# Mixer and stick-breaking in a two-block transformer kernel: exponentials, copies and row norms in other places, a third score buffer

## The reference, cut to what matters

```python
# NSA: compressed, selected and window attention, 6 heads (not touched)
# stick-breaking, 4 heads, causal with s < t
z = (q @ k.T) * scale
log_rest = where(mask, log_sigmoid(-z), 0)
between  = reverse cumulative sum of log_rest, shifted by one
a = where(mask, exp(log_sigmoid(z) + between), 0);  o = a @ v
# HGRN2, 6 heads, chunk by chunk
b = cumsum(log_f);  decay[t, s] = exp(b[t] - b[s]) for s <= t
att = sum_d q[t,d] * key[s,d] * decay[t,s,d]
o = att @ v + (q * exp(b)) @ state
state = exp(b_last) * state + (key * exp(b_last - b)).T @ v
# all mixers: o * silu(gate), then
y = o @ w_out;  x = layer_norm(alpha * x + y) * ln_g + ln_b
```

## Time and profile before

| | us |
|---|---|
| median of 3 runs | 1365.36 |
| lowest, highest | 1359.78, 1369.44 |
| the profiled execution: time | 1365.65 |
| its span, first to last instruction | 1363.9 |
| TensorE busy (share of the span) | 1218.7 (89%) |
| TensorE weight loads | 677.9 (50%) |
| VectorE busy | 538.3 (39%) |
| ScalarE busy | 445.1 (33%) |
| POOL busy | 105.5 (8%) |

### The profile page before, as it was taken

How to read it: one execution, slowest core, us unless ns; L and a number is a source line. 1 busy time by engine, 2 the same in 40 slices (tenths; PEclk the granted TensorE clock), 3 DMA queues, 4 the chain that set the end, 5 groups by cost and what they waited for, 6 DMA issues and landing times.

```text
span 1363.9 us, 16366 instructions
## 1 busy us (share of the span) xinstructions
PE 1218.7 (89%) x5840; PEld 677.9 (50%) x5840; DVE 538.3 (39%) x1412; ACT 445.1 (33%) x1140; POOL 105.5 (8%) x138
## 2 busy tenths in 40 slices
PE   4899989999879898889999989989999899897865
PEld 1565634555554443344555555655454556544542
DVE  3335323334553211235543431112236632665555
ACT  0122324444441012232243312114243544563143
POOL 0000000000020000000000000000000000556342
PEclk8899999999889999989999989989998899888877
DMA  9311444580005302631001005241101111000001
GB/s 349 136 66 31 154 170 140 170 231 1 1 1 123 62 1 62 152 84 69 28 37 62 1 12 134 62 170 47 47 7 41 46 62 62 0 1 32 3 11 53
DMA packets 60406, 99.65 MB, mean 73 GB/s; under 512 B 12084, under 2 KB 22145, under 8 KB 60328
## 3 DMA queue, kind: packets, MB, share of 16 engines
q1 hardware_dynamic: 54514, 93.58, 22.2%
q10 hardware_dynamic: 5814, 5.04, 1.2%
HBM read 96.47 MB, written 4.08 MB: 74 GB/s over the span
## 4 chain that ended last, share of the span: by engine, by line
PE 77%; DVE 11%; ACT 5%; issue 2%; DMA 2%; ACTq 1%; POOL 1%; DVEq 0%; SPq 0%; POOLq 0%
PE PR L911 33%; PE OB L941 6%; PE SC L963 6%; PE PT L804 5%; PE PR L804 5%; PE OB L804 5%; PE SC L804 4%; PE PT L978 3%; PE PR L866 3%; DMA ring<-in_w_ada 2%; PE PR L1002 1%; DVE tok L1800 1%; DVE stage L1800 1%; POOL arena L1710 1%; DVE arena L2025 1%
## 5 line engine op out<-in xcount | busy, mean ns | idle before, releaser
L911 PE MATMUL PR<-ring,hT 128*128 128x512 f32 (+1 forms) x784 | 379.7, 598 | 6.0 <-ACT hT L1270 3.5
L1436 ACT ACTIVATE stage<-stage,nmax 128x256 f32<-128x256 f32 (+7 forms) x200 | 103.7, 519 | 273.1 <-DVE nmax L2158 237.6
L911 PEld LDWEIGHTS PR<-ring,hT 128*128 128x128 f32 x784 | 138.0, 199 | 106.6 <-issue 89.4
L941 PEld LDWEIGHTS OB<-arena,pts 128*128 128x128 f32 (+3 forms) x880 | 130.4, 198 | 97.5 <-issue 76.4
L911 PE MATMUL PR<-hT,ring 128*128 128x512 f32 (+1 forms) x304 | 150.5, 620 | 0.0
L941 PE MATMUL OB<-arena,pts 128*128 128x64 f32 (+4 forms) x880 | 128.5, 274 | 9.0 <-ACT pts L1270 9.0
L1710 POOL TENSOR_TENSOR arena<-arena 128x192 f32<-128x192 f32 (+1 forms) x90 | 60.5, 673 | 823.8 <-PE OB L941 761.4
L963 PE MATMUL SC<-arena 64*128 64x256 f32 (+15 forms) x432 | 113.1, 453 | 4.0 <-DVE nmax L2158 3.6
L978 PEld LDWEIGHTS PT<-ident,stage 128*128 128x128 f32 (+3 forms) x440 | 59.6, 147 | 107.4 <-issue 70.7
L1270 ACT ACTIVATE pts<-PT 128x256 f32<-128x256 f32 (+7 forms) x200 | 80.9, 404 | 84.5 <-PE PT L978 61.4
L978 PE MATMUL PT<-ident,stage 128*128 128x128 f32 (+3 forms) x440 | 86.9, 289 | 22.7 <-DVE stage L1808 10.1
(11 more groups left out here) (374 smaller groups left out, 1331.2 us busy)
## 6 DMA issues: line engine op xcount, KB each, us to landing
ring<-in_w_ada SPq DMA_DIRECT2D x12, 2048.0 KB, 8.3
ring<-in_od_w_in SPq DMA_DIRECT2D x8, 2048.0 KB, 15.1
ring<-in_w_in SPq DMA_DIRECT2D x5, 1536.0 KB, 7.0
ring<-in_ev_w_in SPq DMA_DIRECT2D x3, 2048.0 KB, 10.0
ring<-in_w_in SPq DMA_DIRECT2D x3, 2048.0 KB, 10.4
ring<-in_ev_w_out SPq DMA_DIRECT2D x2, 2048.0 KB, 10.1
ring<-in_od_w_out SPq DMA_DIRECT2D x2, 2048.0 KB, 7.8
ring<-in_w_out SPq DMA_DIRECT2D x2, 2048.0 KB, 7.8
```

Of the source, the lines that this page charges most:

```text
L911: mm = pe.matmul(dst, l, r, start=(k == 0), stop=(k == KT - 1))
L941: mm = pe.matmul(ob[:, h * w:h * w + w], pts[0:rows_, v % 2, n * P:n * P + P], vb, start=(n == 0), stop=(n == len(blocks) - 1))
L1436: give(act.activation(pb[:, s % NP, 0:n], zm[:, s % 2, 0:n], ACT.Exp, bias=nmax[:, row, c:c + 1], scale=-1.0, accum_out=rsum[:, row, c:c + ...
```

## The change

- `OUT_SPREAD` is [2, 5, 5, 0] for chunk 0 (twelve pieces of tile 3's `mE` and `ye`) and [3, 3, 3, 0] for the others.
- Stick-breaking: three score buffers instead of two (`z3` and the two halves of `zm`), picked by `masked_scores`; scores three ahead; VectorE waits for the exponential of s - 3. ScalarE copies the transposes of a stick-breaking step at its start instead of at its end. In the last steps, with no new score, ScalarE's `stick_tail` stands after that copy; VectorE runs the last two tails in step 84.
- Mixer: the four quadrants are written by ScalarE in `cross_blocks`, from a sum that VectorE makes in one instruction; `gm` has two buffers; TensorE waits for `gc_s` alone.
- `exponentials(2)` stands after `cross_blocks(0, 2)` instead of before the chunks, `exponentials(3)` after `cross_blocks(1, 2)` instead of before `cross_blocks(2, 2)`. The POOL runs `differences(2)` before `operands(1)`.
- `mixed_ahead` stands after `cross_blocks(0, 0)`; `norm_sum` one place later in chunks 2 and 3; `norm_scale` ahead of the wait for the outputs; the last `norm_sum` ahead of the mixed copy.
- VectorE runs both `residual_half` before the norm of a chunk's outputs.

```diff
-OUT_SPREAD = [[5, 4, 3, 0], [3, 2, 2, 2]]
+OUT_SPREAD = [[2, 5, 5, 0], [3, 3, 3, 0]]
+STICK_LOOK = 3
...
-        gm = stage[:, 0:2 * GW].rearrange("p (r n) -> p r n", r=2)
+        gm = [stage[:, 2 * GW * n:2 * GW * n + 2 * GW].rearrange("p (r n) -> p r n", r=2) for n in range(2)]
+        z3 = a2["hgt"][:, 0:S]
...
+                ahead = min(need + STICK_LOOK, s_all[-1])
+                if s_units[ahead][2][0] == "sb":
+                    upto = ahead
...
+        def masked_scores(s, n):
+
+            u = s - first_stick
+            if u < 0:
+                return zm[:, s % 2, 0:n]
+            if u % 3 == 0:
+                return z3[:, 0:n]
+            return zm[:, (first_stick + u % 3 - 1) % 2, 0:n]
...
-                    pe.wait_ge(gs_s, n + 1)
                     pe.wait_ge(gc_s, n + 1)
...
+                def transposed(v, sus):
+                    act.wait_ge(pt_done, v + 1)
+                    if v >= 2:
+                        act.wait_ge(pv_done, v - 1)
+                    r, w = transposed_shape(sus[-1])
+                    give(copy(pts[0:r, v % 2, 0:w], PT[v % 2][0:r, 0:w]), pt_ev[v % 2], v // 2 + 1)
+
                 for r_, (v, (_, g, j, sus), new) in enumerate(steps(L)):
+                    if sus[-1][0] == "sb":
+                        transposed(v, sus)
+                    if not new:
+                        stick_tail()
...
-                    if s_units[-1][0] == L and s_no[sus[-1]] + LOOK >= len(s_units) - 1:
-                        stick_tail()
...
+                    if sus[-1][0] != "sb":
+                        transposed(v, sus)
...
                 act.wait_ge(gm_s, n + 1)
+                if n >= 2:
+                    act.wait_ge(ho_done, n - 1)
...
-                give(copy(w[0:64, :, 64:P], G[0:64, :, GW + HB:GW + HB + 64]), gc_s, n + 1)
+                link(copy(w[0:64, :, 64:P], G[0:64, :, GW + HB:GW + HB + 64]))
+                act.wait_ge(gs_s, n + 1)
+                for b in range(P // HB):
+                    u = slice(HB * b, HB * b + HB)
+                    ins = copy(w[u, :, u], gm[n % 2][u, :, 0:HB])
+                    if b < P // HB - 1:
+                        link(ins)
+                give(ins, gc_s, n + 1)
...
-            exponentials(2)
...
                 cross_blocks(c, 0)
-                if c >= 2:
-                    norm_sum(c - 2)
-                cross_blocks(c, 1)
                 if c == 0:
                     for g in range(2):
                         mixed_ahead(T - 1, g)
                 if c >= 2:
+                    norm_sum(c - 2)
+                cross_blocks(c, 1)
+                if c >= 2:
                     norm_square(c - 2)
-                if c == 2:
-                    exponentials(3)
                 cross_blocks(c, 2)
-                if c >= 2:
+                if c < 2:
+                    exponentials(2 + c)
+                else:
                     norm_factor()
+                    norm_scale(c - 2)
...
-                if c >= 2:
-                    norm_scale(c - 2)
+            norm_sum(T - 2)
...
-            norm_sum(T - 2)
...
             differences(1)
+            differences(2)
             operands(1)
-            for c in range(2, T):
-                differences(c)
-                operands(c)
+            operands(2)
+            differences(3)
+            operands(3)
...
                         dve.wait_ge(s_done, s + 1)
-                        if s >= 2:
+                        if s > first_stick:
+                            dve.wait_ge(p_done, s - 2)
+                        elif s >= 2:
                             dve.wait_ge(p_done, s - 1)
...
-                    if s_units[-1][0] == L and s_no[sus[-1]] + LOOK >= len(s_units) - 1:
+                    if new and new[-1] == len(s_units) - 1:
                         stick_tail()
...
-                for b in range(P // HB):
-                    u = slice(HB * b, HB * b + HB)
-                    ins = tt(w[u, :, u], gm[u, :, 0:HB], gm[u, :, 2 * HB:3 * HB], ALU.add)
-                    if b < P // HB - 1:
-                        link(ins)
-                give(ins, gs_s, n + 1)
+                give(tt(p[:, :, 0:HB], p[:, :, 0:HB], p[:, :, 2 * HB:3 * HB], ALU.add), gs_s, n + 1)
...
-                if c:
-                    residual_half(c - 1, 0)
-                else:
-                    for h in range(2):
+                for h in range(2):
+                    if c:
+                        residual_half(c - 1, h)
+                    else:
                         residual_ahead(T - 1, h)
...
-                if c:
-                    residual_half(c - 1, 1)
```

More of the change, by code:

```diff
@@ L607, in steps @@
                 yield v, v_units[v], new
+        first_stick = s_no["sb", 0, 0]
+        def masked_scores(s, n):
[5 more added lines that the diff above has]
+            return zm[:, (first_stick + u % 3 - 1) % 2, 0:n]
         def score_operands(su):
@@ L1407, in stick_tail @@
                         hear(sb_a, "sb_a")
-                        give(act.activation(pb[:, s % NP, 0:n], zm[:, s % 2, 0:n], ACT.Exp), p_done, s + 1)
+                        give(act.activation(pb[:, s % NP, 0:n], masked_scores(s, n), ACT.Exp), p_done, s + 1)
                 def close_behind(v):
@@ L1442, in attention @@
                                                 bias=nmax[:, row, c:c + 1]))
-                    if s_units[-1][0] == L and s_no[sus[-1]] + LOOK >= len(s_units) - 1:
-                        stick_tail()
                     if r_:
                         close_behind(v - 1)
-                    act.wait_ge(pt_done, v + 1)
-                    if v >= 2:
-                        act.wait_ge(pv_done, v - 1)
-                    r, w = transposed_shape(sus[-1])
-                    give(copy(pts[0:r, v % 2, 0:w], PT[v % 2][0:r, 0:w]), pt_ev[v % 2], v // 2 + 1)
+                    if sus[-1][0] != "sb":
+                        transposed(v, sus)
                     if r_ < len(schedule[L][1]):
@@ L2375, in level_sums @@
             def level_sums(n):
-                G, w = GB[n % 2], att[n % 2]
+                G, p = GB[n % 2], gm[n % 2]
                 dve.wait_ge(g_done, n + 1)
                 if n >= 2:
-                    dve.wait_ge(ho_done, n - 1)
-                give(tt(gm, G[:, :, 0:GW], bass.AP(levels.tensor, levels.offset, [list(levels.ap[0]), [0, 2], [1, GW]]),
+                    dve.wait_ge(gc_s, n - 1)
+                give(tt(p, G[:, :, 0:GW], bass.AP(levels.tensor, levels.offset, [list(levels.ap[0]), [0, 2], [1, GW]]),
                         ALU.mult), gm_s, n + 1)
-                link(tt(gm[:, :, 0:3 * HB], gm[:, :, 0:3 * HB], gm[:, :, 3 * HB:6 * HB], ALU.add))
-                link(tt(gm[:, :, 0:HB], gm[:, :, 0:HB], gm[:, :, HB:2 * HB], ALU.add))
-                for b in range(P // HB):
-                    u = slice(HB * b, HB * b + HB)
-                    ins = tt(w[u, :, u], gm[u, :, 0:HB], gm[u, :, 2 * HB:3 * HB], ALU.add)
-                    if b < P // HB - 1:
-                        link(ins)
-                give(ins, gs_s, n + 1)
+                link(tt(p[:, :, 0:3 * HB], p[:, :, 0:3 * HB], p[:, :, 3 * HB:6 * HB], ALU.add))
+                link(tt(p[:, :, 0:HB], p[:, :, 0:HB], p[:, :, HB:2 * HB], ALU.add))
+                give(tt(p[:, :, 0:HB], p[:, :, 0:HB], p[:, :, 2 * HB:3 * HB], ALU.add), gs_s, n + 1)
             residual_ahead(2, 1)
```

6 lines of the change are left out of this document (3 added, 3 removed).

## The result

| | before | after |
|---|---|---|
| median, us (16 runs each) | 1364.51 | 1356.79 |
| lowest, highest | 1359.78, 1369.93 | 1348.81, 1360.11 |
| the profiled execution: time | 1365.65 | 1354.4 |
| its span | 1363.9 | 1352.9 |

The ratio is 0.9932 with a 95% interval of 0.9915 to 0.995: the change is faster by 0.7%, 7.7 us by the medians and 9.3 by the ratio, where 1348 was forecast. (The profiled execution of one experiment, the one with the label f2, was a disturbed one of 3448.84 us, some 2.5 times the other five, so its trace isn't compared with the others.)

A forecast was written before the change was run, and what follows sets the result against it. TensorE's queue was taken as the stick-breaking bound, with about 23 us of waits and slow clock, the mixer as a ring of hand-overs. Gains of 11 + 7 = 18 us off 1365.65 gave 1348, range 1336 to 1360.

The forecast's parts named there:

- Rival A: Whole kernel: time as forecast, 1348 us (1342 to 1353); chance 0.50.
- B: Mixer: the POOL is late, y_s(4) holds everything after chunk 1 and the mixer's gain is eaten; 1354.6 us, chance 0.17.
- C: Stick-breaking gains only 1 us, bound by output-tile copies, each wait bringing back slow clock; mixer gains 7; 1357.6, chance 0.10.
- Step 1: Stick-breaking, first output tile: waits behind exponentials(0) go, mixed copies end at 1188.1 instead of 1193.1; gain 5.1 us.
- Step 2: Stick-breaking, same copies at the second chunk: the wait of 2.44 us stays but for 0.6.
- Step 3: End of stick-breaking: TensorE's 3.61 us bank wait shrinks to 0.3; gain 3.3, plus 3.4 from half clock behind it.
- The half clock in front: Stick-breaking, behind the wait left at the first output tile: a low-clock stretch of some 9 us, 1.4 lost.
- the costing of the quadrant copies: Mixer: four ScalarE copies take 1.0 us; 12 x 1.0 more lie in its gaps; path 1.5 to 2 shorter beside POOL.
- Chunk 0: Mixer: moving mixed_ahead removes a 3.24 us wait, first outputs' wait shortens by 0.6; ends at 18.3, not about 22.1.
- Outputs to norm: Mixer, last norm: chain from outputs to norm takes 6.3 us as today, ending at 87 in place of 92.6.
- D: Slower: the clock stays low after the 4 us wait at 1184; 1375 us if through the whole stretch; chance 0.05.
- E: More gain: shorter waits don't lower the clock and norms meet no POOL piece; 1340 us, chance 0.18.

The follow-up runs named there:

- f2: Changed kernel with quadrants written by VectorE and output spread put back to [3, 2, 2, 2]; other five executions' median 1351.79 us, ratio to before 0.9898.
- s1: Changed kernel with exponentials(0) at the end of step 78 instead of 75, exponentials(1) of 83 instead of 82; ratio to before 0.9912.
- s4: Changed kernel with exponentials(0) at the end of step 78 instead of 75, exponentials(1) of 87 instead of 82; ratio to before 0.9877.
- e6: Changed kernel with the four quadrants written by VectorE again, as four sums, without ScalarE's copies; mixer 106.1 us, ratio to before 0.987.
- f1: Changed kernel with quadrants on VectorE and exponentials(0) and (1) at the ends of steps 78 and 87; 1345.8 us, ratio to before 0.9857.
- e3: Changed kernel with exponentials(2) put back ahead of the chunks; mixer 110.0 us, ratio to before 0.9897.
- e9: Changed kernel with VectorE's first level sums of the next chunk between norm and state update; mixer 114.5 us, ratio to before 0.9944.

## Why the prediction was right in sign and short in size

It said 1348 and a range of 1336 to 1360; 1356.8 is in the range, at its upper end. 18 us were forecast, 9.7 are there in the two stretches. Rival A, as forecast, was bounded by 1342 and 1353 and had a chance of 0.50, and a time under 1351.7 one of 0.67; neither came. What came is the change within 1%, at 0.28; and against the forecast's word that 1% is what can be told from no change, the interval of sixteen runs each tells 0.7% from it. The range holds the time because it was drawn to take in rivals B and C, whose mechanisms weren't at work, so that part is luck. What was right is the direction, the end of stick-breaking and the list of waits that would go.

**Stick-breaking, 11 forecast, 8.0 found.**
- *Step 1 failed* (5.1 forecast). The first products for tile 0 start 116.3 us after M, 117.3 before: 1.0 gained. The step counted ScalarE's own passes and left out that they wait for VectorE. `exponentials(0)` end 106.0 us after M and not at 104.1 ("about 1180"), 1.9 late: in the two steps ahead of them ScalarE waits 1.03 and 1.17 us for VectorE's combinations (at 1172.84 and 1176.36). The three steps behind them take 9.3 us and not 7.2: VectorE had been held with ScalarE (3.04 us), and ScalarE waits for VectorE 0.20, 0.34 and 1.45 us. Both together are the 4.1 us that are missing. s1 and s4 have this place at 111.5, 5.8 us before the kernel before; but there the exponentials no longer stand ahead of the copies, so this isn't the term of step 1.
- *Step 2* (0.6): the wait at the second tile grew from 2.44 to 3.26 us instead; the place comes 1.2 us earlier, of which 1.0 were brought along, so 0.2 gained.
- *Step 3 right* (3.3, and 3.4 for the half clock behind it): the bank wait is gone. The first products of tile 2 start 5.8 us earlier (162.9 and 157.1 after M), 4.6 more than at tile 1, and no half clock follows, which gives 2.2 us from there to T0. Together 6.8, where 6.7 were forecast.
- *The half clock in front*: behind the waits that were left it is some 10 us low (5.64 at 0.75, 4.10 and 2.90 at 0.50), where 9 were forecast; the 5.5 us at 0.53 behind tile 1's longer wait weren't.

**Mixer, 7 forecast, 1.75 found.**

| after T0 | before | forecast | after |
|---|---|---|---|
| end of chunk 0 | 22.1 | 18.3 | 20.5 |
| y_s(4) | | 36 | 36.6 |
| exponentials(3) end | | 39.8 | 40.5 |
| first, last outputs of chunk 1 | 32.3, 39.6 | 26.6, 35.3 | 30.2, 39.1 |
| norm of chunk 1 | 43.7 | 44.3 | 45.4 |
| first, last outputs of chunk 2 | 51.3, 60.0 | 49.9, 60 | 51.9, 61.9 |
| norm of chunk 2 | 66.1 | 65 to 66 | 68.7 |
| first, last outputs of chunk 3 | 78.1, 86.4 | 70.3, 80.7 | 74.1, 83.2 |
| norm of chunk 3 | 92.6 | 87 | 91.0 |

- *The step that failed is the costing of the quadrant copies*: "12 x 1.0 us more on ScalarE lie in its gaps". ScalarE's busy share was no evidence for that: the gaps were waits for VectorE, in the loop that the copies join. Their duration was right (1.11 for four), their place was not free. e6 prices it: 3.8 us, and f1 beside s4: 4.4.
- *Chunk 0* was 2.2 us slow: the ten products behind its level products took 6.81 us, against 4.51 for ten at full clock later in the chunk. Clock by stretch, the first 20 us of the mixer before, after and in f1:

```profile
1252.31:1272.31 20.00, 15.22 (x356) 9.33 (x356) 11.56 (x23) 4.30 (x15) 10.75 (x16) 0.83 0.03 7
1243.05:1263.05 20.00, 17.69 (x364) 10.82 (x364) 5.68 (x15) 10.39 (x29) 4.46 (x7) 0.83 0.03 9
1239.39:1259.39 20.00, 18.26 (x477) 12.37 (x476) 11.50 (x26) 8.29 (x21) 11.94 (x19) 0.91 0.03 9
```

  The clock is no lower than before; the forecast took the wait of 3.24 us out and had no term for the clock behind it. With the same mixer code and 0.91 (s4) or 1.00 (s1), chunk 0's outputs end at 17.8 and 17.5 instead of 19.9, and the mixer takes 109.3 and 108.5: some 0.5 to 1.4 us in the end, so most of a gain in chunk 0 is lost again by the norm of chunk 1 (45.6 and 45.0 beside 45.4). f1, without the copies on ScalarE and with 0.91, gains 6.7 us over before, about the 7 of the sum.
- *Right*: the 8.05 us wait for the POOL is gone, differences(3) at 36 us, exponentials(3) ahead of chunk 1's square, no transposes waiting for an exponential. *Wrong about them*: ScalarE waited 1.48 us for the POOL there, not 5, since it was late itself, and in e3 the mixer is as long without this wait.
- *Outputs to norm*: 6.3 us forecast for chunk 3, by letting "every SBUF-only instruction of the chain wait for the running piece"; 7.8 measured, because the square stood behind the row scaling (1326.09 and 1.24) as well.
- *The end*, 1 us: VectorE's last combination behind the POOL takes 1.28 us, before 3.04; 1.8. But the last six products took 8.00 us instead of 6.86.

**The rivals.** 1356.8 is near C's number (1357.6) and B's (1354.6), and neither mechanism was at work: the stick stretch gained 8.0 and not 1, and an earlier POOL changed nothing (e3, whose stretches are the changed kernel's; its ratio, 0.9897, lies lower, and no stretch shows why). A number that fits is not a cause. D and E didn't come.

## What to carry to other kernels

An engine's idle time is only free if its cause is known: here work moved into gaps that were waits for a partner engine lengthened the loop that both share, and it showed at a row norm that had nothing to do with the edit. A long instruction in an in-order queue holds also those that wait for the queue's next result; put it where the whole queue is idle, and look for the next wait once it is gone (s1). And when a change is worth less than the spread of executions, count from a mark in the unchanged code: here that made differences of 0.1 us readable up to T0, and of some 1 us in the mixer, beside a spread of 10.

## What the runs showed of the hardware

- VectorE's tiny instructions, 0.17 us when free, take 1.29 and 1.77 us beside the POOL's 128x1024 pieces in chunk 2, 1.30 and 1.77 in chunk 3, 0.95 and 0.85 in e6, and end with them to within 0.03 us in all six places: such a block was as long as what was left of the POOL's instruction. Those with one input in PSUM aren't held: at 1290.33 of the changed kernel, beside operands(3), the masking product (stage<-SC,grow) took the 0.56 us that it takes with the POOL idle, and the three SBUF-only sums behind it 1.55 instead of 0.88.
- Identical code ahead of M took between 1068.4 and 1079.3 us in thirteen executions. In these two, e9 and e3, the granted clock of the first 200 us was 0.95 and 0.92; whether the clock is all of it was not tried.
- The last six output products took 8.00 us with a wait of 7.92 us ahead of their transposes, and 8.39 with one of 4.87 (e6): the shorter wait brought its own 3 us, and no faster products.
